# Issue order of the first loads, of the vector loads, and of the x and weight halves in a projection kernel

## What is computed

```python
h = rmsnorm(x, g_pre)
proj = h @ w_in                       # q, k, v_a, o, za, ig, fg, u, vb, zb, ga, gb
q, k = silu(causal_conv4(q, k))       # then chunkwise mLSTM, 8 heads x 256
vb_n = layernorm(vb, ln_g, ln_b)
y_b = u * (tril(w_s) @ vb_n + b_s) * silu(zb)
merged = sigmoid(ga) * (y_a @ w_pa) + sigmoid(gb) * (y_b @ w_pb)
y = x + rmsnorm(merged @ w_out, g_post)
```

## Time and profile before

| what | value |
|---|---|
| median of 3 runs | 1472.92 us |
| profiled execution | 1474.01 us, of which span 1472.5 us |
| PE busy | 1449.1 us (98%) |
| DVE busy | 880.7 us (60%) |
| ACT busy | 627.1 us (43%) |
| POOL busy | 191.3 us (13%) |
| mean load and store rate | 198 GB/s over the span |
| granted clock of PE, mean | 0.992 |

### The profile page before, as it was taken

The page is one execution under the profiler, slowest core; times in us unless marked ns, Lnnn a source line. Parts: engine busy times, 40 slices in busy tenths (PEclk is TensorE's granted clock), DMA queues, the critical chain, the costliest instruction groups (busy, mean ns, idle before and its releaser), DMA issues. The chain is left out here.

```text
span 1472.5 us, 31039 instructions
## 1 busy us (share of the span) xinstructions
PE 1449.1 (98%) x11035; PEld 1426.7 (97%) x11035; DVE 880.7 (60%) x1488; ACT 627.1 (43%) x890; POOL 191.3 (13%) x340
## 2 busy tenths in 40 slices
PE   8999999999999999999999999999999999999996
PEld 8899999999999999999999999999999999999996
DVE  7686656555443437677676767676767544545444
ACT  6343334333333334454545454535353443333442
POOL 4000000002000000413131313131312000000000
PEclk9999999999999999999999999999999999999998
DMA  8464554556655558596969697969796655555543
GB/s 271 160 168 140 158 163 150 176 161 197 211 183 169 186 169 230 165 290 181 294 177 297 174 293 179 301 172 295 179 288 170 216 185 169 184 174 187 173 160 140
DMA packets 311366, 292.13 MB, mean 198 GB/s; under 512 B 82913, under 2 KB 297657, under 8 KB 310657
## 3 DMA queue, kind: packets, MB, share of 16 engines
q1 hardware_dynamic: 292032, 242.79, 56.6%
q0 software_dynamic: 18960, 48.48, 9.6%
q10 hardware_dynamic: 336, 0.37, 0.1%
HBM read 266.12 MB, written 25.44 MB: 198 GB/s over the span
## 5 line engine op out<-in xcount | busy, mean ns | idle before, releaser
L1089 DVE TENSOR_TENSOR wlo<-raw,whi 128x1024 fp32r<-128x1024 f32 x416 | 506.8, 1222 | 514.9 <-ACT whi L823 512.6
L823 ACT ACTIVATE whi<-raw 128x1024 fp32r<-128x1024 f32 x416 | 439.4, 1058 | 680.4 <-PE ps L458 648.7
L456 PE MATMUL ps<-xh,whi 128*128 128x288 f32 x2304 | 684.0, 297 | 2.8 <-DVE xl L1224 2.8
L457 PE MATMUL ps<-xl,whi 128*128 128x288 f32 x2304 | 682.6, 296 | 0.0
L458 PE MATMUL ps<-xh,wlo 128*128 128x288 f32 x2304 | 679.8, 295 | 0.0
L456 PEld LDWEIGHTS ps<-xh,whi 128*128 128x128 f32 x2304 | 434.2, 188 | 7.8 <-DVE xl L1224 3.1
L457 PEld LDWEIGHTS ps<-xl,whi 128*128 128x128 f32 x2304 | 433.8, 188 | 0.4
L458 PEld LDWEIGHTS ps<-xh,wlo 128*128 128x128 f32 x2304 | 433.5, 188 | 0.0
L456 PE MATMUL ps<-yh,whi 128*128 128x288 f32 x768 | 228.5, 298 | 0.0
L457 PE MATMUL ps<-yl,whi 128*128 128x288 f32 x768 | 228.1, 297 | 0.0
L458 PE MATMUL ps<-yh,wlo 128*128 128x288 f32 x768 | 227.3, 296 | 0.0
(11 more groups left out here) (358 smaller groups left out, 1027.2 us busy)
## 6 DMA issues: line engine op xcount, KB each, us to landing
raw<-in_w_in_dram SPq DMA_DIRECT2D x320, 512.0 KB, 3.7
raw<-in_w_pb_dram SPq DMA_DIRECT2D x32, 512.0 KB, 3.2
Cin<-in_state_mlstm_C_dram POOLq DMA_DIRECT2D x16, 1024.0 KB, 8.4
Xb<-in_state_mlstm_C_dram SPq DMA_DIRECT2D x256, 64.0 KB, 3.7
out_dram<-Cin POOLq DMA_DIRECT2D x16, 1024.0 KB, 6.0
raw<-in_w_pa_dram SPq DMA_DIRECT2D x32, 512.0 KB, 3.2
raw<-in_w_out_dram SPq DMA_DIRECT2D x32, 512.0 KB, 3.2
bcs<-rows_d POOLq DMA_DIRECT2D x8, 304.0 KB, 3.7
```

The costliest lines, as they stand in the source:

```text
L456: nc.tensor.matmul(out, whi[:, c, kk, cols], mh_[:, k, :], start=(k == 0), stop=False)
L457: nc.tensor.matmul(out, whi[:, c, kk, cols], ml_[:, k, :], start=False, stop=False)
L823: nc.scalar.activation(whi[:, c], raw[:, c], ACT.Copy).then_inc(hi_ready, 1)
L1089: nc.vector.tensor_tensor(wlo[:, c], raw[:, c], whi[:, c].bitcast(F32), ALU.subtract).then_inc(lo_ready, 1)
```

## The change

`load_pair` asks for quarter c of x ahead of weight chunk c. The second `idle_run` has 16 rounds in place of 3. The transposes of x run three blocks ahead in place of four, and the splits of chunks 1 to 3 of pair 0 stand behind blocks 3, 8, 12 in place of 5, 9, 13. The loads into `prow` move from ACT's queue to POOL's, `turn_par` moves ahead of pair 1, and `parameters` and `x_variance` ahead of the split of pair 2, chunk 0. POOL asks for b_s, ln_g and ln_b behind the stores of m_p and m_s. In pairs 4 to 7 both engines make the x half ahead of the weight half: ACT's step is `xh`, `split_hi`, DVE's is `scaled_x`, `lower_x`, `split_lo`. In pair 8 `split_lo` of pair 9, chunk 0, moves behind the statistics.

```diff
@@ load_pair (SP)
-                sp.dma_start(raw[:, c], w[c, :, :, ds(col, PW)]).then_inc(raw_landed[c], 16)
                 if first:
                     sp.dma_start(xt[:, 0:2, QUARTERS[c]], xp_v[:, :, QUARTERS[c]]).then_inc(x_in[c], 16)
+                sp.dma_start(raw[:, c], w[c, :, :, ds(col, PW)]).then_inc(raw_landed[c], 16)
@@ tensor
-        idle_run(3)
+        idle_run(16)
...
-            pe.wait_ge(w_sp_in, 32)
+            pe.wait_ge(w_sp_in, 16)
...
-            if k + CK < KT:
-                turn_x(k + CK)
+            if k == 2:
+                turn_x(CK)
+            if 2 <= k < KT - 3:
+                turn_x(k + 3)
             pe.wait_ge(x_lo, k + 1)
...
                     if first and (s, c) == (0, 3):
                         gate_sums()
+                        turn_par()
                     if first and (s, c) == (1, 0):
-                        turn_par()
                         turn_w_s()
@@ scalar
-        act.dma_start(prow[:, 0, :], w_conv.rearrange("j (n p) -> (j n) p", p=P)).then_inc(par_in, 16)
-        act.dma_start(prow[0:32, 1, :], b_conv.rearrange("(n p) -> n p", p=P)).then_inc(par_in, 16)
-        act.dma_start(prow[32:48, 1, :], g_pre.rearrange("(n p) -> n p", p=P)).then_inc(par_in, 16)
-        act.dma_start(prow[48:64, 1, :], g_head.rearrange("h (n p) -> (h n) p", p=P)).then_inc(par_in, 16)
...
-            if k % CK == 1 and k > CK:
-                split_hi(0, k // CK, first=True)
+            if k in (3, 8, 12):
+                split_hi(0, (k + 1) // CK, first=True)
...
-                    split_hi(pair + 1, c)
-                    if first and s == 0 and c < 3:
-                        square_x(c)
                     if not (first or second):
                         k = 8 * i - 16 + 4 * s + c
                         act.wait_ge(x_ev, KT + k + 1)
                         nc.scalar.activation(xh[:, ds(k, 1), :], xT[:, ds(k, 1), :], ACT.Copy).then_inc(x_hi, 1)
+                    split_hi(pair + 1, c)
+                    if first and s == 0 and c < 3:
+                        square_x(c)
@@ vector
-            if k % CK == 1 and k > CK:
-                split_lo(0, k // CK)
+            if k in (3, 8, 12):
+                split_lo(0, (k + 1) // CK)
...
                     if scale:
                         scaled_x(k)
+                        lower_x(k)
                     split_lo(V0 + 1 + s + 2 * i, c)
-                    if scale:
-                        lower_x(k)
...
-        v_body(0, {(0, 1, 0): (), (0, 3): (gates_a,), (1, 0): (parameters, w_s_masked, x_variance),
-                   (1, 2): (w_s_blocks, x_diagonals)})
+        v_body(0, {(0, 1, 0): (), (0, 3): (gates_a, parameters, x_variance), (1, 0): (w_s_masked, x_diagonals),
+                   (1, 2): (w_s_blocks,)})
...
             if first:
-                split_lo(G0 + 1, 0)
                 from_turned(1, 7, 7 * PW)
                 layer_norm_stats()
+                split_lo(G0 + 1, 0)
...
-                dve.wait_ge(ln_in, 32)
+                dve.wait_ge(ln_in, 48)
@@ gpsimd: behind the load of m0
+        pool.dma_start(prow[:, 0, :], w_conv.rearrange("j (n p) -> (j n) p", p=P)).then_inc(par_in, 16)
+        pool.dma_start(prow[0:32, 1, :], b_conv.rearrange("(n p) -> n p", p=P)).then_inc(par_in, 16)
+        pool.dma_start(prow[32:48, 1, :], g_pre.rearrange("(n p) -> n p", p=P)).then_inc(par_in, 16)
+        pool.dma_start(prow[48:64, 1, :], g_head.rearrange("h (n p) -> (h n) p", p=P)).then_inc(par_in, 16)
@@ gpsimd: from behind the load of wsn to behind the stores of m_p and m_s
-        pool.dma_start(bsb[:].rearrange("p g t -> p (g t)"), b_s.rearrange("g t -> (g t)").partition_broadcast(P)
-                       ).then_inc(w_sp_in, 16)
-        pool.dma_start(lng[:], ln_g.partition_broadcast(P)).then_inc(ln_in, 16)
-        pool.dma_start(lnb[:], ln_b.partition_broadcast(P)).then_inc(ln_in, 16)
+        pool.dma_start(bsb[:].rearrange("p g t -> p (g t)"), b_s.rearrange("g t -> (g t)").partition_broadcast(P)
+                       ).then_inc(ln_in, 16)
+        pool.dma_start(lng[:], ln_g.partition_broadcast(P)).then_inc(ln_in, 16)
+        pool.dma_start(lnb[:], ln_b.partition_broadcast(P)).then_inc(ln_in, 16)
```

## The result

The changed kernel takes 1479.78 us (median of 6 runs, 1478.15 to 1480.51) against 1474.03 us for the kernel before in its 6 runs: ratio 1.0039, 95% interval 1.0028 to 1.0050. That is 5.8 us more; the forecast was 5.0. (The forecast time of 1477.9 stood on 1472.92, the median of the first 3 runs of the kernel before.) The profiled span is 1478.0 us against 1472.5.

The account below looks back on a forecast made before the run. PE was taken to bound the kernel, busy 1449.1 of 1472.5 us. Terms +4.6 (including -0.1 and -6.1), +0.8 and -0.4 gave +5.0: 1479.0 us like the profiled execution, 1477.9 beside the median; range 1471.5 to 1483.5.

Parts of the forecast that it names:

- First stall: PE's 3.5 us wait in pair 1 and the slow clock behind it, expected to go: -6.1 us.
- Start: Up to the first product, with x asked for first and 16 idle rounds: net -0.1 us.
- the weight chunk at about 7.5: Start: weight chunk 0 lands at about 7.5 us once swapped behind x, so the first product can start near 11.0.
- The ring: Pairs 4 to 7: `scaled_x`, `xh`, `split_hi`, `split_lo` wait in a closed circle, 3.2 us a step, 15.2 a pair.
- x: Delay added to m_s's landing, hence the first `scaled_x`, by b_s, ln_g, ln_b and pair 5's chunks: 2 us taken.
- Waits for `vf`: PE stands about 0.7, 2 and 2 us at the transposes of pairs 4 to 6, inside the same lateness.
- Pair 8 at 142.05: Forecast start of pair 8 after the ring, against 137.41 before: +4.6 us.
- Slow clock: Behind the last wait, of about 7 us, at pair 8: +0.8 us, between 0 and 1.5.
- `vn`: Pair 8: `from_turned` ahead of the split brings it 1.5 us forward, ending PE's 0.4 us wait: -0.4 us.
- the two sides: Rival, 0.20: ring there, but m_s no later or the start gives its 0.6; 1474.4 to 1475.8 us.
- The order did not do what it says: Denies the 0.14 rival: x halves done before the last weight split, pair 8 following pair 7 directly; 1463 to 1465 us.
- The starved chunks: Rival, 0.12: pair 5's weight chunks starve beside the three loads, x is 5 to 8; 1481 to 1484 us.

Follow-up runs that it names:

- The two runs at the end: Old order, vector loads spaced out, weight chunk first, 9 idle rounds, pair 7's x blocks sooner: 1461.82 us; that kernel with x first and 16 idle rounds: 1463.56 us.

## Why the prediction was right

The sign, the size (5.0 forecast, 5.8 measured) and the mechanism held. Term by term:

- *First stall, -6.1.* Right: 6.5. From the end of chunk 1 of pair 1 to the transposes in pair 2 PE takes 14.0 us (40.85 to 54.81) in place of 20.5 (39.87 to 60.32).
- *Start, -0.1.* Wrong in sign. The step that failed is "the weight chunk at about 7.5": it landed at 8.8, so the first product came at 12.12 in place of 11.0, 0.7 us later than before, and by 40 us PE is 1.0 behind (40.85 against 39.87). Start and first stall together are 5.5 us in place of 6.2 (the same `split_lo` at 52.99 and 58.48). The two runs at the end put 1.7 us on x first together with the longer idle run. The clock did stay at 1.00, but the transposes of x were done at 10.2, ahead of what the first product waited for, so it won nothing. The recorded working is also loose here: 32 records at 0.16 from 4.86 would end at 9.9 and not at 9.2; they took 0.12 each and ended at 8.9.
- *The ring, 3.2 us a step and 15.2 a pair.* Measured 3.17 and 15.1 (107.48 to 122.54 from pair to pair). 59.3 forecast for the whole, 59.2 found. The run with the new order alone and the runs with either half put back show that it is the order, and which half.
- *x, +2.* Right size, cause mostly wrong. m_s landed 9.8 us after its issue in place of 8.0, but it also took 9.5 with the loads elsewhere. The loads are worth 0.7 us at pair 8. Against the 5.5 us that had been gained ahead, the first `scaled_x` is 1.75 us late (83.20 against 81.45).
- *Waits for `vf` of 0.7, 2 and 2.* Found 2.7, 1.6 and 1.6, and as said within the lateness.
- *Pair 8 at 142.05.* Found 142.4, after a wait of 6.8 us (7 forecast). *Slow clock +0.8*: found +1.1. *`vn` -0.4*: the wait is gone.

The rivals: the two sides did not cancel. The order did not do what it says: `xh` waits for `scaled_x` in all 16 steps. The starved chunks were there, and worse than the prediction's bound of 12.5 us. One chunk of pair 5 in the changed kernel (KB, us to landing), asked for at 76.6:

```profile
raw<-in_w_in_dram SPq DMA_DIRECT2D x1, 512.0 KB, 16.7
```

It cost ACT only 0.3 us because the ring brought ACT there late, not because the ring asked for it late: with the order put back it was asked for at 76.4 and cost 6.9. So that this rival stayed small is in part luck: it rests on the ring being there, not on the loads doing little. The time of the three loads was also misread: 2.6 MB at the 0.35 MB a microsecond of the earlier trace rows are 7.5 us and not 10.5, and in the changed kernel the last of them landed 18.6 us after the first was asked for (73.78 to 92.4). Here are the DMA queues at 88 to 89 us of that kernel (packets, MB, share), and then the only queue with packets at 82 to 86:

```profile
q0 software_dynamic: 50, 0.36, 87.9%
q1 hardware_dynamic: 49, 0.05, 14.6%
```
```profile
q0 software_dynamic: 89, 0.61, 53.8%
```

At 88 us it is packet for packet again, at seven times the bytes. The Trainium skill, page DMA: Bandwidth & Descriptors, section Queues, rings and completion order, says that an engine takes turns between queues by packets; in this microsecond the trace agrees, 50 to 49. It does not in others: from 78 to 86 us SP's queue moved no packet, though the chunk asked for at 76.6 had not landed, and in the kernel before none from 29 to 32 us, beside the chunk that took 12.5. So turns by packets do not explain these landings alone; what held SP's queue back in those stretches is open.

What was missing from the reasoning: that DVE's half alone is a ring as well, of 2.70 us. It decided nothing in the forecast, but the run came 3.6 us above the range that I had expected for it (1473.06 against 1469.5).

## What to carry to other kernels

Before moving an instruction ahead of another on one of two engines that feed each other, go round the circle: if each engine's next step stands behind something that waits for the other, add up the hops; that sum per step against the pace of the engine that sets the end was the core of this forecast. To have something ready sooner, move it to a step with room, not ahead of the work that lets the engines run apart. And test a small gain in a kernel that has no later wait: the slow clock behind such a wait came and went from trace to trace, by more than the gain.

## What the runs showed of the hardware that was not expected

A store of 64 values of 4 bytes each took 8.0 to 10.8 us to land in the twelve kernels that have it, and for some 4 us cut what all queues move from 258 to 98 GB/s. The Trainium skill, page DMA: Bandwidth & Descriptors, section Specifications, says that transfers under 512 B are done as read-modify-write; the runs show the slowness, not how it comes about.

SP's queue moved no packet for 3 us (kernel before, 29 to 32) and 8 us (changed kernel, 78 to 86) while POOL's queue did and a weight chunk was still to land.

The same wait of PE (2.84 us) was followed by a first chunk of 4.65 us in one kernel and 5.93 in another, where 3.2 to 3.3 is the time at the upper clock. Behind a wait of 1.96 us the granted clock fell to 0.50, and behind one of 2.92 us it stayed at 1.00. At the start, where the kernel before and the one with the new order alone run the same code, the first transposes of x ran at a granted clock of 0.54 in one trace (behind a wait of 2.06 us) and 1.00 in the other (1.62 us). So the price of a short wait varies by more than a microsecond from trace to trace, as much as some of the edits measured here, and one trace of each kernel does not tell what of it belongs to the kernel.
